# The latent weights loaded ahead of x's later tiles, and tile 0's latent products made ahead of tile 1's turning, in the opening of a two-layer encoder step

## What is computed

```python
def rmsnorm(x, g, eps=NORM_EPS):
    xf = x.astype(jnp.float32)
    y = xf * lax.rsqrt(jnp.mean(xf * xf, axis=-1, keepdims=True) + eps)
    return (y * g.astype(jnp.float32)).astype(x.dtype)
...
    proj = rmsnorm(x, norm_mix) @ w_in
    p_a, p_b = proj[..., :A_COLS], proj[..., A_COLS:]
    o_a, ckv, krope = mla_mixer(p_a, qpos, kpos, cache_ckv, cache_krope,
                                a_q_norm, a_w_uq, a_kv_norm, a_w_ukv, a_q_gain, a_k_gain)
    o_b, shift, wkv = rwkv7_mixer(p_b, ...)
    x = x + jnp.concatenate([o_a, o_b], axis=-1) @ w_out
...
    x = x + peer_ffn(rmsnorm(x, norm_ffn), p_wq, p_keys, p_u, p_v)
```

## Time and profile before

| | us |
|---|---|
| median of 3 runs | 3728.5 |
| lowest and highest of them | 3721.72, 3731.05 |
| profiled execution, time | 3727.73 |
| profiled execution, span of the core | 3725.9 |

### The profile page before, as it was taken

One profiled execution on the slowest core, in us unless ns is written; L12 is line 12 of the kernel. 1 busy time (PEld: TensorE's weight loads), 2 busy tenths in 40 slices (PEclk: granted clock), 3 DMA queues, 4 the chain that ended last, 5 costly groups with the idle time before them and its releaser, 6 DMA issues.

```text
span 3725.9 us, 33994 instructions
## 1 busy us (share of the span) xinstructions
PE 3066.2 (82%) x9408; PEld 1506.9 (40%) x9408; DVE 2662.6 (71%) x6446; ACT 1350.9 (36%) x4001; POOL 1438.4 (39%) x1241
## 2 busy tenths in 40 slices
PE   8997996988777777989898878888988877777777
PEld 5765994333232322444343433333433322322222
DVE  2676665887666667789988576899867667666664
ACT  3354221233333333324573232346633333333332
POOL 1211002454444444444345344453444344444442
PEclk9997997999899999999999999999999999999999
DMA  4100016999999999999999999999999999999998
GB/s 130 38 14 1 1 46 226 419 415 418 413 421 418 420 407 411 416 416 385 348 377 410 379 421 418 421 412 355 408 421 421 401 421 422 421 418 407 421 415 349
DMA packets 216557, 1293.13 MB, mean 347 GB/s; under 512 B 23600, under 2 KB 41008, under 8 KB 68784
## 3 DMA queue, kind: packets, MB, share of 16 engines
q0 software_dynamic: 165888, 1208.03, 79.0%
q1 hardware_dynamic: 50480, 82.93, 6.4%
HBM read 1286.49 MB, written 3.87 MB: 346 GB/s over the span
## 4 chain that ended last, share of the span: by engine, by line
DMA 42%; PE 20%; DVE 11%; issue 8%; ACT 3%; POOL 1%; DVEq 0%; SPq 0%; ACTq 0%; POOLq 0%
DMA ring<-in_uv,route 41%; PE banks L1647 15%; DVE ring L1587 4%; DVE X L1597 2%; ACT route L1632 1%; PE banks L2035 1%; PE banks L2027 1%; DVE own L2283 1%; ACT route L1617 1%; PE banks L1975 1%; PE banks L2001 1%; ACT route L1622 0%; POOL ring L1576 0%; DMA own<-in_l_peer_wq 0%; DMA own<-in_l_w_out 0%
## 5 line engine op out<-in xcount | busy, mean ns | idle before, releaser
L1647 PE MATMUL banks<-ring,route 128*128 128x512 f32 (+1 forms) x4088 | 1993.7, 624 | 553.3 <-ACT route L1632 531.7
L1576 POOL DMA_INDIRECT ring<-in_uv,route x1152 | 1322.7, 1148 | 1706.8 <-PE banks L1647 1506.0
L1587 DVE SCALAR_TENSOR_TENSOR ring<-ring,XN 128x1024 f32<-128x1024 f32 x1152 | 1408.6, 1223 | 731.5 <-DMA ring<-in_uv,route 720.0
L1647 PEld LDWEIGHTS banks<-ring,route 128*128 128x128 f32 (+1 forms) x4088 | 728.6, 189 | 1649.5 <-issue 849.0
L1617 ACT ACTIVATE route<-route 128x2 f32<-128x2 f32 x576 | 117.3, 204 | 1864.0 <-DVE ring L1587 1863.6
L1632 ACT ACTIVATE route<-IDN,route 128x128 f32<-128x128 f32 x894 | 309.3, 387 | 3.8 <-PE banks L1647 2.6
L1622 ACT ACTIVATE route<-route 128x1 f32<-128x1 f32 x1152 | 276.6, 287 | 23.2
L1975 PE MATMUL banks<-own,QP 128*128 128x512 f32 (+1 forms) x400 | 176.2, 564 | 5.3 <-DMA own<-in_l_w_in 3.1
L1597 DVE SCALAR_TENSOR_TENSOR X<-ring,route,X 128x1024 f32<-128x1024 f32 x130 | 166.4, 1280 | 0.9
L1617 ACT ACT_TABLE_LOAD x106 | 136.0, 1283 | 1.9
L1975 PEld LDWEIGHTS banks<-own,QP 128*128 128x128 f32 x400 | 76.3, 192 | 94.2 <-issue 82.0
(11 more groups left out here) (503 smaller groups left out, 3360.1 us busy)
## 6 DMA issues: line engine op xcount, KB each, us to landing
ring<-in_uv,route POOLq DMA_INDIRECT x1152
own<-in_l_w_in SPq DMA_DIRECT2D x16, 1024.0 KB
own<-in_l_w_out SPq DMA_DIRECT2D x12, 1024.0 KB
own<-in_l_peer_wq SPq DMA_DIRECT2D x12, 1024.0 KB
X<-in_x_prompt SPq DMA_DIRECT2D x8, 512.0 KB, 6.3
ring<-in_l_w_in SPq DMA_DIRECT2D x4, 1024.0 KB, 9.7
ring<-in_l_peer_wq SPq DMA_DIRECT2D x2, 2048.0 KB, 11.9
own<-in_l_w_in SPq DMA_DIRECT2D x4, 656.0 KB
```

Of the source, the lines that this page charges most:

```text
L1576: pool.indirect_dma_start(self.ring[:, s % RING, :], None, self.io[f"uv{of_slot(s)[0]}"], bass.IndirectOffsetOnAxis(ap=self.EI[:, g % 2, k ...
L1587: dve.scalar_tensor_tensor(u, u, 1.0, self.XN[:, of_slot(s)[1], :], ALU.mult, ALU.mult, accum_out=self.HD[:, g % 2, k:k + 1]).then_inc(sel ...
L1647: m = pe.matmul(self.bank[1 + half][0:n, :], self.DG[:, (V_TENSOR[s] - 1) % 4, 0:n], self.ring[:, s % RING, D + 512 * half:D + 512 * half ...
```

## The change

Two things are moved, and nothing is added or removed. In SP's list the load of the latent weights `WA` (1664 KB) takes the place of `BV`'s (21 KB) behind the identity, so that it stands ahead of x's tiles 1 to 4; `BV` takes the place that `WA` had. In `front_order()` the entry ("a", 0) moves ahead of ("x", 1), which moves it in the lists of TensorE and ScalarE alike. VectorE's and GpSimd's lists stay as they are.

```diff
@@ -342,7 +342,7 @@
 def front_order():
 
-    order = [("x", 0), ("x", 1), ("a", 0), ("x", 2), ("a", 1), ("x", 3), ("a", 2), ("x", 4), ("a", 3), ("a", 4)]
+    order = [("x", 0), ("a", 0), ("x", 1), ("x", 2), ("a", 1), ("x", 3), ("a", 2), ("x", 4), ("a", 3), ("a", 4)]
     order += [("b", n) for n in range(3)]
@@ -432,13 +432,13 @@
             x_tile(0, xl[0])
             sp.dma_start(gain, io["l0_norm_mix"].partition_broadcast(P)).then_inc(xl[0].h, 16)
             sp.dma_start(IDN[:, :], io["idn"]).then_inc(xl[0].h, 16)
-            sp.dma_start(BV[:, :], io["bvec"]).then_inc(bv.h, 16)
+            sp.dma_start(WA, wv[:, :, 0:ACOLS]).then_inc(wa.h, 16)
             x_tile(1, xl[1])
             x_tile(2, xl[2])
             x_tile(3, xl[3])
             sp.wait_ge(xz.h, xz.at(1))
             sp.dma_start(X[0:DEC, 4, :], io["x_sample"][0]).then_inc(xl[4].h, 16)
-            sp.dma_start(WA, wv[:, :, 0:ACOLS]).then_inc(wa.h, 16)
+            sp.dma_start(BV[:, :], io["bvec"]).then_inc(bv.h, 16)
             for i in range(4):
                 slab(sp, i)
```

## The result

The changed kernel takes 3735.58 us in the median of 22 runs (3730.54 to 3738.39), against 3726.95 for the kernel before (22 runs, 3721.72 to 3731.4): a ratio of 1.0021 with a 95% interval of 1.0015 to 1.0027. It is 8.6 us slower. The prediction was 8.0 us slower, 3736.5 us, and no change by the bound of 0.3%, which holds too. The profiled execution has a span of 3734.1 us, 8.2 more than before.

What follows compares the result with a forecast made beforehand. TensorE, 82% busy, was taken to set the pace after an opening held by landings and engine lists. 5.8 (including 0.3) + 2.1 = 7.9, called 8.0 us, gave 3736.5 us, range 3728 to 3744.

Steps and rivals of the forecast that it cites:

- The first step: Opening: WA's transfer delays tile 1's landing to 12.5, which holds up tile 0 through VectorE's list; products 0.3 us later.
- The second step: Tile 2's turning waits for tile 3's square behind the copy of tile 0's products: 5.8 us late, 0.3 included.
- The clock: TensorE behind the 4 us pause ahead of tile 2's turning: slow restart costs 2.1 us more.
- One for one to the end: After the opening: no later wait swallows the shift, so the front's whole delay reaches the kernel's end.
- (a): Loads: tile 1 is not held up as transfers share engines; still no gain, 3732.1 us; chance 0.08.
- (b): Opening: faster, tile 0's products using TensorE's idle time at full clock; gain 1 or 2 us at most, 3727; chance 0.04.
- (c): After the opening: a later wait tied to something fixed swallows the shift; 3728.5 us; chance 0.08.
- (d): TensorE's clock stays down through both first bursts: 12 to 14 us slower, some 3741 us; chance 0.15.

Runs made afterwards that it cites:

- the run with the load alone: Changed kernel with the written order of before, only WA's load moved ahead of x's tiles 1 to 4: 3730.7 us, ratio 1.0011.
- the square ahead: Changed kernel with ScalarE's square of tile 3 right behind that of tile 2, before the copy of tile 0's products: 3729.24 us, ratio 1.0005.
- the look-ahead gone: Changed kernel with VectorE making each tile's mean right ahead of its own scaling, not one tile ahead: 3726.49 us, ratio 0.9998.
- the filled pause: Changed kernel with five unread matmuls on TensorE behind tile 1's turning: 3734.53 us, ratio 1.0021; again 3732.61 us, ratio 1.0014.
- the unhooked lists: Changed kernel, VectorE's means right before their own scalings, ScalarE's copies of tile 0 before later squares, tile 1's before tile 0's products: 3723.09 us, ratio 0.9990.

## Why the prediction was right

**The size.** 8.0 us was forecast and 8.6 measured (7.8 in the repeat). Both stalls were worked out from the lists of the engines and the landings, and both are in the trace where they were put. That the places agree to a few tenths is in part luck: the prediction was worked out from one execution of before, in which tile 1 landed at 8.2 and `WA` at 17.1. In the three other profiles with these loads in their old places tile 1's square started at 8.5 to 8.6, and `WA` landed at 18.0 to 18.5.

**The first step** (tile 1's landing holds up tile 0) was right in mechanism: the run with the load alone shows it. Its size was 0.8 and not 0.3, because tile 1 landed at 13.0 and not at 12.5. A cause for these 0.5 us is not shown. ScalarE's first square, released by the identity's load ahead of `WA`, was 0.46 later too (7.16, not 6.70), but in the three other profiles with the loads in their old places it was earlier (6.05 to 6.36), and tile 1 later than 8.2 all the same. The scatter alone is as large as the step: beside the second profile of before, whose products start at 18.32, those of the changed kernel (18.34) are not late at all.

**The second step** (the square of tile 3 behind the copy of tile 0's products) was right to a tenth. From the copy to tile 2's turning was forecast as 4.95 us, and 31.01 - 26.06 is 4.95. The runs with the square ahead and with the look-ahead gone each take this pause away, one from each end of the wait. The prediction had named both, the square's place and the mean of the next tile ahead of this one's scaling; the runs add that each is needed.

**The clock** was taken as 2.1 between bounds of 0 and 3.2; the filled pause measures 2.3, the repeat of the changed kernel 1.7 (30.98 to 39.39 is 8.4 us, against 6.7). In the three other profiles with the pause of 4.1 us the same stretch took 9.1 to 9.4, so the loss was 1.7 to 2.7 in all five. The table's 6.5 and 2.0 divide the same 8.5 a little differently: in stride the first weight load of a turning starts 0.35 ahead of its matmul (24.52 and 24.87), behind a pause together with it (31.01), so that by the matmuls it is 6.1 for the pause and 2.4 for the clock. The rule of the Trainium skill that the prediction weighed, in TensorE: Matmul & The Clock Gate, "Why this matters for your kernels", is borne out by these five profiles.

**One for one to the end** holds on the whole: 8.5 late at the second mixer's products, 8.7 at the next block, 8.2 in the span, 8.6 in the median. For single executions it does not hold to better than about 2 us, as the last section shows: the second profile of before was 1.4 later than the first at the second mixer's products and 0.1 later at the next block.

**The rivals.** (a) has no part: tile 1 was held up by the full transfer, and when its load was put first, the opening was 4.6 us later all the same. (b) did not come, but the mechanism that it named, TensorE's idle time ahead of the products, is what the unhooked lists use: its ceiling was given as 1 or 2 us, and they gain 3.2 in the opening, since the ceiling was worked out with the stall behind the copy left in. (c) falls by the row at 214.16: the shift is still there. (d) did not come: tile 0's products took 7.7 us (7.34 before), and behind the pause the clock was back up before tile 3's turning (39.84), so that tile 2's products took the 5.75 of the stride.

## What to carry to other kernels

Before an early step is moved up, read every engine's list for what stands ahead of the work that it needs: here a look-ahead of one tile in one list and a square in another tied tile 0 to the landing of tile 1, and tile 2 to the products of tile 0. A bigger load put ahead of a small one that a look-ahead waits for delays what stands behind that wait by its own transfer, even if its data comes on time. And a reordering that opens a pause on TensorE can pay for the pause and then for the slow clock behind it, here 1.7 to 2.7 us behind each pause of 4.1. And a repeat of the kernel before is worth its time early: single profiles of it differ by 1.4 us at the yardstick.

## What the runs showed of the hardware

**The slow start of TensorE varies.** Tile 0's products, the same 16 pieces, took 7.23 to 8.82 us in the fourteen profiles, the two ends being the unhooked run and the second one with the pause filled. Two executions of one kernel differ by up to 1.5 us (7.36 and 8.82 with the pause filled). The Trainium skill, TensorE: Matmul & The Clock Gate, Part 1 on the clock gate, states that the number of slow matmuls at a start differs from run to run. The trace agrees: of the single weight loads behind the first two, three took 0.34 us in the one execution, and eight in the other.

**The same short pause sometimes costs nothing.** Every profile has the pause of 2.6 us ahead of the first turned heads. In three of the fourteen profiles, the load-alone run, the first one with the pause filled and the second of before, the eight pieces behind it took 2.75 us; in the other eleven 3.38 to 4.44, and 4.44 in the first profile of before. The load-alone run:

```profile
92.91 1.08 PE L540 MATMUL banks<-IDN,X 128*96 128x128 f32 x8 [2.58 <-DVE X L749]
93.82 2.75 PE L529 MATMUL banks<-X,own 128*128 128x384 f32 x8
```

That is 1.7 us, by which a run can win back part of its delay: the load-alone run is 5.1 late at the second mixer's products and 3.3 at the next block. What decides between the two was not tried.

**The first loads landed later with `WA` behind them.** ScalarE's first square is released by the identity's landing. It started at 6.05 to 6.70 in the four profiles in which the small `BV` load stands behind the identity, and at 6.87 to 7.26 in the eight in which `WA` does. With tile 1's load there it was 7.24 and 6.25, so that one order of the loads gave 1.0 us of scatter by itself. The mechanism was not tried.
